# First layer's queries and keys of x made by channel, and another order of the first quarters

## The reference, cut to what matters

```python
hx = modulate(rmsnorm(x, pre_mix_g[i]), sh1, sc1)      # sh1, sc1 from cx @ ada_w[i] + ada_b[i]
hc = modulate(rmsnorm(h_ctx, pre_mix_g[i]), csh1, csc1)
...
def mlstm_project(h, w_in, b_in):
    hk, hv = M_HEADS * M_DK, M_HEADS * M_DV             # 4 * 128, 4 * 256
    p = h @ w_in + b_in
    q, k, v, o, gates = jnp.split(p, [hk, 2 * hk, 2 * hk + hv, 2 * hk + 2 * hv], axis=-1)
    q = heads(q, M_DK)
    k = heads(k, M_DK) * (M_DK ** -0.5)
...
    s = jnp.einsum('bhtd,bhsd->bhts', qc, kc) * jnp.exp(dmat - m_t[..., None])   # needs q, k of x
    C_new = a * C + jnp.einsum('bhs,bhsd,bhse->bhde', ws, kc, vc)                # needs k of the context
```

## Time and profile before

| | |
|---|---|
| median of three runs | 805.65 us |
| the profiled execution, own time | 805.81 us |
| its span (first to last instruction) | 803.7 us |
| PE busy | 776.0 us, 97% of the span |
| VectorE (DVE) busy | 547.1 us, 68% |
| ScalarE (ACT) busy | 415.0 us, 52% |
| DMA in the first 50 us | about one, as a share of the 16 engines' time |

### The profile page before, as it was taken

The page is one execution under the profiler, slowest core; times in us unless marked ns, Lnnn a source line. Parts: engine busy times, 40 slices in busy tenths (PEclk is TensorE's granted clock), DMA queues, the critical chain, the costliest instruction groups (busy, mean ns, idle before and its releaser), DMA issues. The chain is left out here.

```text
span 803.7 us, 11764 instructions
## 1 busy us (share of the span) xinstructions
PE 776.0 (97%) x4579; PEld 664.7 (83%) x4579; DVE 547.1 (68%) x722; ACT 415.0 (52%) x581; POOL 95.1 (12%) x155
## 2 busy tenths in 40 slices
PE   6999999999999999999989999999999999999996
PEld 5777877777789898888789988988888898988874
DVE  2586699876777878877577785654567767664465
ACT  3533322634676676635366555456465454543264
POOL 4100401311200000000070313210100000000010
PEclk9999999999999999999999999999999999999999
DMA  9976676814276555588445342221457555645611
GB/s 308 361 259 221 214 243 230 294 52 144 80 236 209 179 171 181 200 262 315 157 117 176 105 158 69 100 95 53 154 188 228 191 194 172 206 151 193 225 64 52
DMA packets 107902, 144.84 MB, mean 180 GB/s; under 512 B 6344, under 2 KB 70353, under 8 KB 107857
## 3 DMA queue, kind: packets, MB, share of 16 engines
q1 hardware_dynamic: 100512, 137.38, 51.3%
q10 hardware_dynamic: 7280, 6.83, 2.7%
q0 software_dynamic: 64, 0.01, 0.0%
HBM read 142.10 MB, written 2.10 MB: 179 GB/s over the span
## 5 line engine op out<-in xcount | busy, mean ns | idle before, releaser
L1284 DVE TENSOR_TENSOR w_lo<-raw,w_hi 128x2048 fp32r<-128x2048 f32 (+1 forms) x61 | 135.8, 2230 | 66.6 <-ACT w_hi L672 66.4
L2087 PE MATMUL ps<-h_parts,w_hi 128*128 128x512 f32 x504 | 179.6, 396 | 0.0
L672 ACT CAST w_hi<-raw 128x2048 fp32r<-128x2048 f32 (+1 forms) x61 | 113.0, 1853 | 83.2 <-PE ps L1963 56.3
L2086 PE MATMUL ps<-h_parts,w_lo 128*128 128x256 f32 x504 | 140.6, 279 | 0.0
L2087 PEld LDWEIGHTS ps<-h_parts,w_hi 128*128 128x128 f32 x504 | 94.6, 188 | 19.4
L1292 DVE TENSOR_TENSOR w_lo<-raw,w_hi 128x2048 fp32r<-128x2048 f32 x44 | 100.7, 2289 | 7.4 <-ACT w_hi L680 7.1
L2086 PEld LDWEIGHTS ps<-h_parts,w_lo 128*128 128x128 f32 x504 | 95.0, 189 | 3.3
L680 ACT CAST w_hi<-raw 128x2048 fp32r<-128x2048 f32 x44 | 84.0, 1909 | 0.0
L1961 PE MATMUL ps<-w_hi,act_hi 128*128 128x512 f32 x176 | 69.0, 392 | 0.0
L1963 PE MATMUL ps<-w_hi,act_lo 128*128 128x512 f32 x176 | 68.5, 389 | 0.0
L1962 PE MATMUL ps<-w_lo,act_hi 128*128 128x512 f32 x176 | 68.5, 389 | 0.0
(11 more groups left out here) (424 smaller groups left out, 1555.2 us busy)
## 6 DMA issues: line engine op xcount, KB each, us to landing
raw<-in_ffn_up_w SPq DMA_DIRECT2D x22, 1024.0 KB, 5.1
raw<-in_w_gate_up SPq DMA_DIRECT2D x22, 1024.0 KB, 5.1
raw<-in_ada_w SPq DMA_DIRECT2D x16, 1024.0 KB, 5.2
raw<-in_w_in SPq DMA_DIRECT2D x14, 1024.0 KB, 5.3
raw<-in_m_in_w SPq DMA_DIRECT2D x11, 1024.0 KB, 5.2
raw<-in_ffn_down_w SPq DMA_DIRECT2D x10, 1024.0 KB, 5.3
raw<-in_w_down SPq DMA_DIRECT2D x10, 1024.0 KB, 5.0
raw<-in_m_out_w SPq DMA_DIRECT2D x4, 1024.0 KB, 5.1
```

Source lines behind the costliest of these rows:

```text
L672: act.copy(part_view(w_hi, s), raw_view(split[s])).then_inc(hi_ready, 1)
L1284: dve.tensor_tensor(part_view(w_lo, s), raw_view(split[s]), part_view(w_hi, s).bitcast(F32), ALU.subtract).then_inc(lo_ready, 1)
L2086: pe.matmul(both[:, 0], lo[:, k, w], h_hi[:, k, :], start=False, stop=False)
L2087: ins = pe.matmul(both, hi[:, k, w], h_parts[:, :, k, :], start=False, stop=k == KD - 1)
```

## The change

`part` for x now lets 128 columns of the weights (one head f) stand and streams 256 tokens: 4 heads x 2 blocks x 3 products = 24 matmuls of 256 columns. The result lies by channel. ACT writes it straight to `qkT` with the bias as a column: keys after the last `keys_c`, queries after the last `queries`. The 16 transposes, DVE's additions for k and q of x, and one bias load go. DVE's additions for the context's keys stay. The small sums over `lf` are spread over the heads of `queries(3)`. Two loads of 4 x 128 biases and one small DVE operation (`q_bias`) come in. In the first quarters PE, ACT and DVE get another order, and far behind `fsum_out(1)` moves ahead of `gdn_silu(3)`.

```diff
@@ part @@
+                if want == "x":
+                    banks = [ps[:, sources + f // 2, f % 2 * T:(f % 2 + 1) * T] for f in range(MH)]
+                    for f in range(MH):
+                        c = slice(f * DK, (f + 1) * DK)
+                        for k in (2 * q, 2 * q + 1):
+                            pe.matmul(banks[f], hi[:, k % 4, c], h_hi[:, k, :], start=k == 0 and f % 2 == 0, stop=False)
+                            pe.matmul(banks[f], lo[:, k % 4, c], h_hi[:, k, :], start=False, stop=False)
+                        if between is not None:
+                            between(f)
+                    pe.wait_ge(S("hT"), FIRST_ORDER[want][q])
+                    for f in range(MH):
...
+                            ins = pe.matmul(banks[f], hi[:, k % 4, c], h_lo[:, k, :], start=False,
+                                            stop=k == KD - 1 and f % 2 == 1)
@@ PE @@
             ada1_group(0)
-            ada1_group(1)
-            pe.wait_ge(S("last_in"), 16)
-            first_transposed(0, 0)
             pe.wait_ge(S("vec_in"), 16 * (len(VEC) + 3))
...
+            pe.wait_ge(S("last_in"), 16)
+            first_transposed(0, 0, (0,))
+            ada1_group(1)
+            first_transposed(0, 0, (1,))
+            ada1_columns(0)
             first_transposed(0, 1)
-            ada1_columns(0)
             first_transposed(0, 2)
-            first_transposed(0, 3)
...
             ada1_group(2)
+            first_transposed(0, 3)
             ada1_group(3)
...
-            queries(3, (1,)).then_inc(group_used, 1)
+            queries(3, forget_sums_of).then_inc(group_used, 1)
             exponent_rows()
-            def qk_by_channel():
...
-                            ins = flip(ps[:, 5 + h % 2, a * T + t * P:a * T + (t + 1) * P],
-                                       qk_tok[:, a, t, h * DK:(h + 1) * DK])
@@ ACT @@
             gate_rows_out(1, P, 2 * T)
+            act.wait_ge(group_used, at["k"][1] + 1)
+            for h in range(MH):
+                act.activation(qkT[:, h, 1, :], ps[:, h // 2, h % 2 * T:(h % 2 + 1) * T], ACT.Identity,
+                               bias=pcol("k_bias", h)).then_inc(S("qkT_ready"), 1)
...
+            act.wait_ge(group_used, at["q"][1] + 1)
+            for h in range(MH):
+                act.activation(qkT[:, h, 0, :], ps[:, 5 + h // 2, h % 2 * T:(h % 2 + 1) * T], ACT.Identity, scale=DK ** -0.5,
+                               bias=q_bias[:, h:h + 1]).then_inc(S("qkT_ready"), 1)
@@ ACT, second block @@
             gdn_mid(3)
+            fsum_out(1)
             gdn_silu(3)
             act.wait_ge(S("p_stored"), 32)
             token_squares(0)
             token_squares(1)
-            fsum_out(1)
@@ DVE @@
             lo_until(2)
-            lo_until(3)
             for q in (2, 3):
                 ada1_rows(q)
-                if q == 3:
-                    lo_until(4)
+                lo_until(q + 1)
                 modulation(q)
```

More of the change, by code:

```diff
@@ L775, in _, with x_copy @@
                 sum_sq(x[:, t, :], SS["norm1"] + t)
-            for i in range(4):
+            def x_copy(i):
                 act.wait_ge(S("tr"), i + 1)
@@ L780, in _ @@
                     .then_inc(S("x_out"), 1)
[L781 to L784, removed]
+            bias_cols = (MH * DK, 2 * MH * DK, 2 * MH * DK + NB, 2 * MH * DK + MH * DV, 2 * MH * DK + MH * DV + NB)
             def load_bias(i):
@@ L808, in hi_c @@
                 act.copy(c_hi[:, 2 * i:2 * i + 2, :], cfull[:, 2 * i:2 * i + 2, :]).then_inc(S("hi"), 1)
+            act.wait_ge(S("first_half"), 16)
+            act.copy(part_view(w_hi, 0)[:, 0:2, :], raw_view(0)[:, 0:2, :]).then_inc(S("first_half"), 1)
+            x_copy(0)
+            x_copy(1)
             hi_x(0)
+            x_copy(2)
             act.wait_ge(S("ctx_in"), 16)
@@ L853, in _ @@
             act.copy(mw[0:MH].rearrange("p v d t -> p (v d t)"), junk[0:MH, :]).then_inc(S("w_row"), 1)
-            act.wait_ge(S("kq_done"), 6)
-            load_bias(3)
             hi_until(6)
[L858 to L862, removed]
             act.wait_ge(S("m_cols_out"), 1)
@@ L1417, in keys_lo @@
                                   ALU.subtract).then_inc(want, 1)
+            first_diagonals(0)
+            dve.wait_ge(S("vec_T"), 4)
+            dve.tensor_copy(cols[:], ps[:, 7, 2 * KD:2 * KD + n_col]).then_inc(S("vec_T"), 1)
+            ada1_rows(0)
+            keys_lo(0, S("first_half"), 17, S("first_half"))
+            dve.wait_ge(S("vec_T"), 5)
             modulation(0)
             scale_x(0)
-            keys_lo(0, S("first_half"), 17, S("first_half"))
             lo_x(0)
+            link(dve.tensor_scalar(q_bias[:], cols[:, col["q_bias"]:col["q_bias"] + MH], DK ** -0.5, None, ALU.mult))
             first_diagonals(1)
             ada1_rows(1)
+            keys_lo(1, hi_ready, 1, lo_ready)
             modulation(1)
             scale_x(1)
-            keys_lo(1, hi_ready, 1, lo_ready)
             s_next[0] = 1
@@ L1465, in _ @@
             dve.wait_ge(group_used, at["k"][1] + 1)
-            for i, dst in enumerate((qk_tok[:, 1, 0, :], qk_tok[:, 1, 1, :], k_ctx[:, 0, :], k_ctx[:, 1, :])):
-                dve.tensor_tensor(dst, ps[:, i, :], bias_of(0), ALU.add).then_inc(S("kq_done"), 1)
+            for t in range(TT):
+                dve.tensor_tensor(k_ctx[:, t, :], ps[:, TT + t, :], bias_of(0), ALU.add).then_inc(S("kq_done"), 1)
             dve.wait_ge(S("gate_sums"), 1)
@@ L2180, in ada1_columns, with first_transposed @@
                 ins.then_inc(S("ada_T"), 1)
-            def first_transposed(c, i):
+            def first_transposed(c, i, halves=(0, 1)):
                 if c:
                     pe.wait_ge(S("x_out"), 4)
-                for k in (2 * i, 2 * i + 1):
+                for k in (2 * i + j for j in halves):
                     for t in range(TT):
@@ L2246, in _, with part @@
             every = [(*X0, 0), (*X1, 1), (*C0, 2), (*C1, 3)]
-            def part(name, q, sources, want="c"):
+            def part(name, q, sources, want="c", between=None):
                 s = at[name][q // 2]
@@ L2269, in keys_x, with queries @@
             def keys_x(q):
-                return part("k", q, every[:TT], "x")
+                return part("k", q, 0, "x")
             def keys_c(q):
                 return part("k", q, every[TT:], "c")
-            def queries(q, tiles=(0, 1)):
-                return part("q", q, [((*X0, 5), (*X1, 6))[t] for t in tiles], "x")
+            def queries(q, between=None):
+                return part("q", q, 5, "x", between)
             keys_x(0)
             ada1_group(2)
+            first_transposed(0, 3)
             ada1_group(3)
@@ L2282, in _ @@
             first_transposed(1, 0)
+            ada1_columns(1)
             first_transposed(1, 1)
-            ada1_columns(1)
             first_transposed(1, 2)
@@ L2308, in _, with forget_sums_of @@
             queries(2)
-            queries(3, (0,))
-            pe.wait_ge(S("lf_ready"), 1)
             def lf_of(tile, d):
                 return lf[:, 2 * tile + d, :]
-            for a in range(2):
+            def forget_sums_of(a):
+                if a == 0:
+                    pe.wait_ge(S("lf_ready"), 1)
+                if a == TT:
+                    for d in range(2):
+                        for t in range(TT):
+                            ins = pe.matmul(ps[0:MH, 4, 32 + d:33 + d], lf_of(TT + t, d), ones[:, 0:1], start=t == 0, stop=t == 1)
+                    ins.then_inc(S("gate_sums"), 1)
+                if a >= TT:
+                    return
                 sums = ps[:, 4, 16 * a:16 * a + 16].rearrange("p (t d h) -> p d t h", t=TT, d=2)
@@ L2324, in _ @@
                     pe.matmul(sums[:, d, t, :], ones[:], lf_of(TT * a + 1 - t, d), start=False, stop=True)
[L2325 to L2328, removed]
             def exponent_rows():
@@ L2337, in exponent_rows, with rows_by_token @@
                 ins.then_inc(S("gate_sums"), 1)
-            queries(3, (1,)).then_inc(group_used, 1)
+            queries(3, forget_sums_of).then_inc(group_used, 1)
             exponent_rows()
-            def qk_by_channel():
[L2344 to L2349, removed]
-                            ins = flip(ps[:, 5 + h % 2, a * T + t * P:a * T + (t + 1) * P],
-                                       qk_tok[:, a, t, h * DK:(h + 1) * DK])
-                    ins.then_inc(S("qk_T"), 1)
+            def rows_by_token():
                 pe.wait_ge(S("mrow_ready"), 2)
```

39 lines of the change are left out of this document (19 added, 20 removed).

## The result

The changed kernel takes 809.15 us, the median of 7 runs (807.77 to 811.53), against 805.65 us for the kernel before. The ratio is 1.0051, with a 95% interval of 1.0035 to 1.0067: 4.1 us slower, where I forecast 2.5 us faster. The profiled execution took 811.53 us, so it lies at the upper end of the runs.

The account below looks back on a forecast made before the run. PE, working through 97% of the span, was taken as the bound. Terms 2.0 - 0.5 - 0.3 - 1.2 + 2.5 + 0 + 0 gave 2.5 us gained: forecast 803.2 us, range 801.2 to 805.3.

Parts of the forecast that it names:

- The clock: Half-speed stretch at 70 to 80 us, losing 1.7 us: taken as unchanged, 0; rival that it goes, 1.5 us gained, 25%.
- The wait for `lf`: PE at the first small sum would newly wait 1.1 to 1.5 us for ACT's `lf`; 1.2 us lost.
- The first quarters: New order on PE, ACT and DVE up to `keys_x(3)` would start it earlier; 2.0 us gained, lower bound 0.4.
- The sign of error that I had named: Forecast wrong if PE waits on the vectors near 12 to 15 us for more than a microsecond.
- The modulation's wait for PE's columns: In the first quarters, the modulation's 0.82 us wait for PE's columns would go, with PE early.
- The mark of 52.5 us: `keys_x(3)` would start at about 52.5 us instead of 54.59.
- the chain that I called the bound: First quarters: steps behind the fourth weight group's landing at 46.1 us, through `hi_x(3)`, would allow 2.1 us gained.
- Downstream of the first stage: After the first v block, DVE's run moves with PE, and PE's 1.5 us wait at `ctx_state` stays.
- my third rival: DVE's own backlog up to `ctx_state` grows PE's 1.5 us wait to 4: 805.7 us, no change; 9%.
- Pitch: New 256-column matmuls at 0.120 us each: eight quarters cost 0.17 us more each, 1.4 us in all.
- transposes: Removing PE's transposes of 86.84 to 89.32 us gains all their time, 2.48 us, taken as 2.5.
- `fsum_out(1)`: Moving it ends PE's 1.1 us wait, which turns up again at two later places; 0, upper bound 1.1 us gained.

Follow-up runs that it names:

- long_wait: `shift256` with ACT's four key copies made a second time into unused columns, lengthening PE's wait for `lf`; ratio 1.0045 to the kernel before, 810.03 us.
- shift256: Changed kernel, same instructions, with `cols` widened so the tiles behind it lie 256 bytes off their place in the kernel before; ratio 0.9998, 804.40 us.
- order_only: Kernel before, addresses unchanged, with only the new order of the first quarters on PE, ACT and DVE; ratio 0.9978, 804.33 us.
- keys_late256: `shift256` with ACT's four key copies moved behind the exponential and the logarithm; ratio 0.9980 to the kernel before, 803.82 us.
- warm: `keys_late256` with four unused 512-column products behind the first modulation group; ratio 0.9968 to the kernel before, 802.95 us.

## Why the prediction was wrong

- **Addresses: not a term of the sum at all.** I costed every instruction that the change adds, moves or removes, and took the rest of the program as unchanged. The 64 bytes by which two small allocations moved 72 tiles cost 3.9 us in the kernel before and 4.3 us here. This is the larger part of the 6.6 us between forecast and result, and it turns the sign: without it the changed kernel is at 0.9998 with a median of 804.40 us, inside my range, though 2.3 us of the forecast gain are still missing. The next four points are about these.
- **The clock: "a wait of 1.2 us now stands ahead of the sums, so PE does less, not more, around them; I take 0".** The observation was right and the conclusion wrong. In the profile the stretch lost 3.4 us instead of 1.7, outside my bounds of 0 to 1.5 us gained. Over many runs wait and clock together cost 1.5 to 2.3 us, where I had 1.2; that the clock makes the difference is borne out by the profiles together and by `long_wait`, not by each pair. The slower side was priced nowhere but as "a little of a longer half-speed stretch".
- **The wait for `lf`: right mechanism, its size 0.8 instead of 1.2.** The two DMA issues ran beside the copies, which themselves took 1.6 us (65.56 to 67.14) where I had 1.1 to 1.5.
- **The first quarters: right way, size not settled.** The order is worth 1.8 us for 2.0 in the kernel before, but 1.0 us in the channel form, and at `keys_x(3)`, where I priced it, 1.3 us. The profile of the changed kernel hides it: the stretch at 0.57 from 14 to 22 us took 3.4 us from PE, and `keys_x(3)` came at 54.82. The sign of error that I had named, a wait of over 1 us for the vectors, was no sign: `shift256` waits 2.2 us for them and still has `keys_x(3)` at 53.27, since this wait only takes the place of the 2.2 us for `qTw`. The modulation's wait for PE's columns that I took away is still there in the changed kernel, 0.94 us. The mark of 52.5 us was missed by 0.8 even in `shift256`, and there not by the chain that I called the bound: ACT's `hi_x(3)` was done at 52.6 us, as forecast. PE was late. It had no wait from 19.3 us on; its idle time ahead of `keys_x(3)` fell by 2.7 us, from 8.4 to 5.6, but its work took 1.4 us more where I had 0.85. First the modulation's wait in the changed kernel, then `hi_x(3)` in `shift256`:

```profile
52.04 0.36 DVE L1374 TENSOR_TENSOR mod<-ps,cols 128x4 f32<-128x4 f32 x2 [0.94 <-PE ps L2178]
```
```profile
51.98 0.62 ACT L803 CAST h_parts<-full 128x512 fp32r<-128x512 f32 x1 [4.11 <-DVE full L1386]
```

- **Downstream of the first stage: "the 1.5 us stay as they are".** They are 1.7 us, and ahead of them, near 125 to 130 us, PE now waits for DVE's additions to v: 0.7 us in the changed kernel, 1.2 in `shift256` (below), 0.4 in `order_only`, none in the kernel before. So a part of what PE gained is taken back by DVE, the mechanism of my third rival in a smaller size. No experiment isolates what it costs.

```profile
PE ps L1960 <- DVE r L1525: 1.2, 1, 1.2
```

- **Pitch, transposes, `fsum_out(1)`: nothing against them.** The pitch is 0.120 us; the rows' transposes follow the first v group directly. The channel form less its wait is worth 0.6 us for 0.8, but its interval runs from 1.6 us gained to 0.6 lost, so it shows no gain. The move showed none.

The parts come near the whole: -1.8 (order) - 0.6 (channel) + 1.5 to 2.3 (wait and clock) + 3.9 to 4.3 (addresses) give 3.0 to 4.2 us, and 4.1 were measured. With order and channel form taken together, as `keys_late256` has them (-1.6), it is 3.8 to 5.0. Each part is uncertain by 1 us or more, so this is no sharp test.

## What to carry to other kernels

When a change adds or widens a tile, compare the addresses of all tiles behind it, and the duration of untouched matmuls in both traces, before anything else is explained; here padding that puts them 256 bytes off their old place gave some 4 us back, for 192 bytes more in each partition. On an engine that is the bound, a new wait may cost more than its length: here 0.8 us cost 1.5 to 2.3, probably through the clock behind it, and moving four copies past one logarithm removed it. The version to keep is the change with padded `cols` and the key copies behind the logarithm, `keys_late256`, 0.9980 of the kernel before; `warm`, with the four unused products, measured 0.9968, which isn't clearly better.

## What the runs showed of the hardware that I had not expected

- The time of a 512-column float32r matmul depends on the distance between the tiles of its operands: 389 ns at 0 and 256 bytes off the old one, 396 at 64, 393 at 128, and 388, 392 and 394 for three groups at 192; with all tiles moved together by 64 bytes it stays 389. At 64 bytes this is 3.7 us between the first and last of 528 such matmuls.
- The granted clock differs between executions of one kernel: mean clocks of `shift256` went from 0.982 (810.98 us) to 0.997 (803.3 us). A profile is one draw: that of the kernel before (0.996) was above its mean of 0.993 to 0.994. Ten of the 17 profiles have one more stretch at half speed, far from the change, with 0.91 from 400 to 420 us; those of the kernel before and of the changed one have 1.00 there.
- A wait of 2.3 us on PE that ended at 70.4 us was followed by a clock of 0.50 from 70 to 80 us, one of 0.8 us that ended at 70.6 by 0.51 from 72 to 79 us in the changed kernel and by none in `shift256`.
